# A decoder sample's attention spread over three head slots of the dense tiles' expert search

## What is computed

```python
s = jnp.einsum('bqhd,bkhd->bhqk', q, k) * scale   # + forget bias, + mask
p = jax.nn.softmax(s, axis=-1)
o = jnp.einsum('bhqk,bkhd->bqhd', p, v)           # for each of the 8 samples
...
q  = (xb @ w_pq).reshape(128, 8, 256)             # _peer, one 128-frame block
s1 = jnp.einsum('thd,hnd->thn', q[..., :128], sub_keys[0])
s2 = jnp.einsum('thd,hnd->thn', q[..., 128:], sub_keys[1])
v1, i1 = lax.top_k(s1, 16);  v2, i2 = lax.top_k(s2, 16)
cand = v1[..., :, None] + v2[..., None, :]
sv, si = lax.top_k(cand.reshape(128, 8, 256), 16)
```

## Time and profile before

| | us |
|---|---|
| median of 3 runs (1957.52 to 1961.84) | 1957.95 |
| the profiled execution, whole time | 1963.01 |
| its span, first to last instruction | 1961.2 |
| busy: PE 90%, DVE 82%, ACT 41%, POOL 50% of the span | |
| the stage: first query matmul to the turn of the choices | 357.1 to 605.8 |

### The profile page before, as it was taken

One profiled execution on the slowest core, in us unless ns is written; L12 is line 12 of the kernel. 1 busy time (PEld: TensorE's weight loads), 2 busy tenths in 40 slices (PEclk: granted clock), 3 DMA queues, 4 the chain that ended last, 5 costly groups with the idle time before them and its releaser, 6 DMA issues.

```text
span 1961.2 us, 28368 instructions
## 1 busy us (share of the span) xinstructions
PE 1766.0 (90%) x9239; PEld 1486.5 (76%) x9239; DVE 1603.1 (82%) x3321; ACT 803.9 (41%) x1314; POOL 974.2 (50%) x779
## 2 busy tenths in 40 slices
PE   6999989877795876739999999999999999999998
PEld 4883554656644866629999999999999999999997
DVE  5306462477758799999999999999999999999999
ACT  4312661333314554623444344344434443444443
POOL 0004000033213022157777777777777777777773
PEclk8999999888777989969999999999999999999999
DMA  6110303333212443549999999999999999999996
GB/s 246 43 63 2 129 1 123 115 100 100 72 43 86 153 142 124 172 165 417 415 398 412 389 393 400 411 391 392 407 405 393 391 405 403 390 400 407 395 393 273
DMA packets 169005, 517.87 MB, mean 264 GB/s; under 512 B 18128, under 2 KB 51856, under 8 KB 164848
## 3 DMA queue, kind: packets, MB, share of 16 engines
q0 software_dynamic: 73728, 268.47, 34.3%
q1 hardware_dynamic: 70448, 223.46, 30.0%
q10 hardware_dynamic: 24768, 25.17, 3.7%
HBM read 486.20 MB, written 30.84 MB: 264 GB/s over the span
## 4 chain that ended last, share of the span: by engine, by line
PE 77%; DVE 16%; ACT 5%; issue 2%; DMA 1%; SPq 0%; ACTq 0%; DVEq 0%
PE ps L1295 27%; PE ps L1311 9%; PE ps L1313 9%; PE ps L1312 9%; PE ps L1145 3%; DVE asel L1583 2%; DVE bsel L1576 2%; PE ps L984 2%; PE ps L985 2%; PE ps L986 2%; PE ps L1184 1%; PE ps L1233 1%; PE ps L1091 1%; PE ps L1201 1%; PE ps L1104 1%
## 5 line engine op out<-in xcount | busy, mean ns | idle before, releaser
L628 POOL DMA_INDIRECT ubuf<-in_peer_u,ix x256 | 388.3, 1517 | 156.2 <-POOL ix L673 109.1
L628 POOL DMA_INDIRECT vbuf<-in_peer_v,ix x256 | 406.4, 1588 | 78.9 <-issue 77.7
L1311 PE MATMUL ps<-hh,uh 128*128 128x384 f32 x1024 | 346.4, 338 | 18.9 <-DVEq L1694 18.9
L1313 PE MATMUL ps<-hh,ul 128*128 128x384 f32 x1024 | 345.6, 337 | 0.0
L1312 PE MATMUL ps<-hl,uh 128*128 128x384 f32 x1024 | 344.2, 336 | 0.0
L1706 DVE SCALAR_TENSOR_TENSOR ubuf<-ubuf,h2Y 128x1024 f32<-128x1024 f32 x256 | 302.7, 1220 | 3.5 <-DMA ubuf<-in_peer_u,ix 2.8
L930 ACT ACTIVATE vh<-vb 128x1024 fp32r<-128x1024 f32 x128 | 135.9, 1062 | 299.0 <-PE ps L1295 287.6
L1295 PE MATMUL ps<-vl,acth 128*128 128x512 f32 x774 | 243.2, 395 | 0.0
L1295 PE MATMUL ps<-vh,actl 128*128 128x512 f32 x774 | 242.6, 394 | 0.0
L1295 PE MATMUL ps<-vh,acth 128*128 128x512 f32 x774 | 242.6, 394 | 0.0
L1311 PEld LDWEIGHTS ps<-hh,uh 128*128 128x128 f32 x1024 | 193.7, 189 | 25.3 <-issue 19.7
(11 more groups left out here) (367 smaller groups left out, 2948.4 us busy)
## 6 DMA issues: line engine op xcount, KB each, us to landing
ub<-in_peer_uT SPq DMA_DIRECT2D x130, 512.0 KB, 6.7
vb<-in_peer_v SPq DMA_DIRECT2D x129, 512.0 KB, 6.5
gbuf<-gate_matrix SPq DMA_DIRECT2D x68, 384.0 KB
gate_matrix<-stage ACTq DMA_DIRECT2D x12, 2048.0 KB, 7.8
wpqX<-in_wpq SPq DMA_DIRECT2D x8, 1024.0 KB, 4.9
wpqY<-in_wpq SPq DMA_DIRECT2D x8, 1024.0 KB, 5.0
w_oX<-in_w_o SPq DMA_DIRECT2D x4, 1024.0 KB, 8.1
kTs<-in_past_k SPq DMA_DIRECT2D x8, 512.0 KB, 4.0
```

The lines of the kernel that those rows point to most:

```text
L628: nc.gpsimd.indirect_dma_start(out=dst[slot][:, e, :], out_offset=None, in_=t_in[table], in_offset=bass.IndirectOffsetOnAxis(ix[:, slot, e ...
L1311: mm(ps[:, 6 + slot, 0:NTD], uh[slot][:, k], hh[:, k], start=(k == 0), stop=False)
L1313: last = mm(ps[:, 6 + slot, 0:NTD], ul[s][:, k], hh[:, k], start=False, stop=(k == KD - 1))
```

## The change

No instruction is added or dropped; three queues get another order.

- PE: `transpose_probabilities(h - 1)` moves behind `key_scores(h)`, to the end of the head. `sample_values` of sample h - 2 moves between the halves of the queries of head h, so a sample's values come one head later than its transposition. `turn_rows(h - 2)` moves behind the queries.
- ACT: `copy_rows(h - 2)` moves ahead of `copy_queries`, `copy_scores` ahead of `copy_transposed`.
- DVE: `normalise` leaves the end of the iteration. For a sample of odd number it stands in the next iteration behind four items of `half_choices`, for one of even number inside `pair_choices` behind its first eight items (a scaling, the candidates, six maxima). Both halves of `low_weights` stand ahead of `row_max`. Behind a pair (h = 3, 5, 7), the first half and `copy_out` stand behind only four items.

```diff
@@ ACT
             for h in range(PH):
                 if h + 1 < PH:
                     round_weights(h + 1, 0)
+                if h >= 2:
+                    copy_rows(h - 2)
                 copy_queries(0, h)
                 if h + 1 < PH:
                     round_weights(h + 1, 1)
+                copy_scores(0, h)
                 if h >= 1:
                     copy_transposed(FIRST + h - 1)
-                copy_scores(0, h)
                 exponentials(FIRST + h)
-                if h >= 1:
-                    copy_rows(h - 1)
+            copy_rows(DB - 2)
@@ PE
             for h in range(PH):
-                queries(0, h, (lambda: turn_rows(h - 2)) if h >= 2 else None)
+                queries(0, h, (lambda: sample_values(h - 2)) if h >= 2 else None)
+                if h >= 2:
+                    turn_rows(h - 2)
                 scores(FIRST + h)
+                key_scores(0, h)
                 if h >= 1:
                     transpose_probabilities(FIRST + h - 1)
-                key_scores(0, h)
-                if h >= 1:
-                    sample_values(h - 1)
+            sample_values(DB - 2)
             project_out(TD)
@@ DVE
             low_weights(1, 0)
-            normalise(FIRST)
             low_weights(1, 1)
             for h in range(1, PH + 1):
                 items = half_choices(0, h - 1)
-                some(items, 14)
-                if h >= 2:
+                behind_pair = h % 2 == 1 and h > 1
+                some(items, 4)
+                if not behind_pair:
+                    normalise(FIRST + h - 1)
+                else:
+                    if h + 1 < PH:
+                        low_weights(h + 1, 0)
+                    copy_out(FIRST + h - 2)
+                some(items, 8)
+                if not behind_pair and h + 1 < PH:
+                    low_weights(h + 1, 0)
+                some(items, 4)
+                if not behind_pair and h >= 2:
                     copy_out(FIRST + h - 2)
                 if h + 1 < PH:
-                    low_weights(h + 1, 0)
-                some(items, 6)
+                    low_weights(h + 1, 1)
+                some(items, 4)
                 if h < PH:
                     row_max(FIRST + h)
-                some(items, 4)
-                if h < PH:
-                    normalise(FIRST + h)
-                if h + 1 < PH:
-                    low_weights(h + 1, 1)
                 finish(items)
...
                 if h % 2 == 0:
-                    finish(pair_choices(0, h // 2 - 1))
+                    items = pair_choices(0, h // 2 - 1)
+                    some(items, 8)
+                    if h < PH:
+                        normalise(FIRST + h)
+                    finish(items)
```

## The result

The changed kernel takes 1929.49 us (median of four runs, 1927.88 to 1932.49) beside 1957.74 for the kernel before: a ratio of 0.9844, 95% interval 0.9831 to 0.9857, or 28 to 33 us. Measured again beside the experiments, it gave 0.9841 (0.9827 to 0.9854). The forecast was a gain of 37.6 us, to 1920. The profiled execution took 1932.49, its span 1930.7.

A forecast was written before the change was run, and what follows sets the result against it. Neither PE nor DVE fills a stretch; they wait for each other in turn. 418.5 + 41 + 41 + 45.7 puts the last `onehot2X` at 546.2, 37.6 us earlier: 1957.95 - 37.6 = 1920 us, range 1910 to 1936.

The forecast's parts named there:

- the stage: Part of the kernel from 357.1 to 605.8 us, holding all that the change moves; forecast gain 37.6 us.
- the first milestone: DVE's first of four `onehot2X`, one per pair of heads: forecast at 418.5 instead of 424.02, 5.5 us earlier.
- the forecast's own band of 1915 to 1926: Whole kernel time around the forecast of 1920 us; chance 0.60.
- a clock that stays low long: Rival: PE's half clock lasts 15.4 us after each wait, gain only 23.7, 1934 us; chance 0.15 for 1926 to 1938.
- the middle stretches: First to second and second to third `onehot2X` of DVE: forecast 41 us each, before 49.4 and 54.4.
- the walk: Adding measured lengths along the new waits, from one `onehot2X` (time T) to the next: T + 39.9 at full clock.
- half a `low_weights`: DVE term behind a pair, ahead of `copy_out`: 1.15 us, so PE's transposes start at T + 6.3, T being the `onehot2X`.
- nothing waits for new keys: Forecast wait of PE before scores of samples 4 and 6: arrives T + 17.8, goes on T + 20.0 after POOL's decode.
- DVE's 38 us: DVE's work from one `onehot2X` to the next, taken as unchanged; nothing shorter than 38 us was held possible.
- The rule: GpSimd shares SBUF access with VectorE; a denser DVE would stretch POOL's decode, 6 us more, 1926 us; rival's chance 0.05.
- the same 6 us of half clock after each wait: PE's clock loss behind its wait before the transposes: cost 0.9 us per middle pair, last forecast 45.7 instead of 42.7.
- the last stretch: Third to last `onehot2X` of DVE, with the output projection on PE: forecast 45.7 us, 42.7 at full clock.

The follow-up runs named there:

- the faster kernel: Changed kernel with both `low_weights` halves and `copy_out` ahead of the one-hots, new keys ahead of the decode, odd normalising behind 12 items: 1924.17 us (0.9807).

## Why the prediction was right and wrong

**Sign, place and rough size were right.** The gain is all in the stage, and the first milestone came 6.1 us earlier for the 5.5 forecast. But 1929.5 lies above the forecast's own band of 1915 to 1926, in the one of 1926 to 1938 that was kept for a clock that stays low long. In the middle stretches it was not that: with the clock held at 1.00 they stayed at 43.1. The number fell into that band for another reason, and it lies inside the range because the range was wide.

**Half of the miss lies outside the walk.** Of the 9.4 us between the forecast gain and the measured one (28.3 by the medians), the stage accounts for 4.5. The late start of the stage is 1.7 (in the second profile of the changed kernel it began at 357.05 instead of 358.84, so this varies from one execution to the next), the time behind it 0.9. The other 2.3 come from taking the gain of one execution off the median: that execution lay 5.3 us above the median before and 3.0 after.

**The step that failed is a term of the middle stretches: half a `low_weights`, 1.15 us in the walk from T to T + 6.1.** It was priced by the row at 412.00, 1.22 long, when POOL was idle. In its new place it stands beside POOL's product and took 3.60, so the transposes began at T + 8.6 instead of T + 6.3. The second half, which the walk left inside DVE's 38 us, took 3.15. With both, DVE has 41.9 us of work, its gaps of about 1 us between dependent instructions come on top, and no path through PE matters any more. In the run without POOL's products, the same order gave 40.0 and 38.9, and PE's wait was 3.9: with that term at its price, the walk, forecast at 39.9 without a loss of clock, came out. That is in part luck, for two terms changed places: nothing waits for new keys there (2.2 us in the walk), and PE still comes to those scores at T + 20.2 and T + 19.1 instead of T + 17.8, made late by half clock.

**The row for the right price was there.** The earlier trace rows hold the same instruction twice: 1.22 at 412.00 and 1.59 at 433.15. The longer one is the one beside POOL's work. I should have asked why, and taken its worst case, the length of POOL's instruction (4.80 and 3.45), as the upper bound. The first half alone would then have been bounded at 1.2 + 4.8.

**The rule was weighed in one direction only.** The earlier trace rows show a product of 4.80 beside 3.45, and the prediction made of it that POOL would be stretched by a denser DVE. POOL's two products hardly changed (4.79 and 3.51), and its first decode as a whole, from the first product to the first copy of new keys, took 18.17 us instead of 17.20; what was stretched was DVE. The trace of the changed kernel shows both directions: the first product, asked for while `onehotX` was being built, ends 3.35 us after DVE has gone on from `onehotX` to the reciprocal (422.94 to 426.29), a product's own length; and each half of `low_weights` ends one length after the product. POOL's additions behind each product, which meet that half, took 4.31 and 4.34 here and 3.45 in the third pair, where no half is left.

The Trainium skill, SBUF — State Buffer, section SBUF: two separate sides, says just this: the port pair that VectorE and GpSimd share is an exclusive lock, and the instruction that starts first keeps it for its whole length while the other is blocked. The trace agrees, 3.60 and 3.15 for 1.22.

**The wait for the new keys** (2 us in the forecast) is not in the trace after, for PE came to those scores at T + 21.5, behind the keys. Where the halves were moved away it appeared as 0.25 and 0.40: PE, slowed by its half clock, was there at about T + 19, not T + 17.8. It was a true wait but a small one.

**The clock** was costed with the same 6 us of half clock after each wait. In the middle stretches it was 3.2 and some 4.5 us and cost nothing, since DVE was the bound (filling the wait left 43.1). In the last stretch it was more. These stretches of the changed kernel begin where the transposes do:

```profile
428.20:431.40 3.20, 3.20 (x13) 3.04 (x14) 3.17 (x25) 0.85 (x2) 2.96 (x6) 0.51 0.00 0
...
510.62:513.50 2.88, 1.94 (x14) 1.34 (x18) 2.85 (x22) 0.85 (x2) 2.80 (x2) 0.50 0.02 6
513.50:518.00 4.50, 4.50 (x31) 2.66 (x21) 4.27 (x26) 1.37 (x2) 4.26 (x6) 0.50 0.01 2
518.00:524.00 6.00, 6.00 (x13) 2.42 (x12) 5.85 (x24) 1.13 (x5) 5.53 (x6) 0.83 0.00 0
```

(The clock is the number before the last two; 0.50 is 1.2 GHz.) After a wait of 6.29 us it stood at half for some 3.2 us; after one of 3.71, with a second one of 0.94 close behind, for some 9. The forecast went by the length of the wait, and that was the wrong guide. In the last stretch 3.0 us were forecast and 4.0 measured, most of what that stretch missed.

**Costed at nothing** were the moves of `copy_rows`, `sample_values` and the loads, and none of them shows. Not named at all was that the row maxima come behind both halves of `low_weights`. Here it cost nothing, because DVE was the bound; in the faster kernel it cost 3 us.

**The odd normalising** meets POOL as well. For sample 7, in the last stretch, it takes 2.58 us in the changed kernel and 0.63 in the run without POOL's products, which has the same order:

```profile
519.20 2.58 DVE L1438 TENSOR_SCALAR probS<-probS,stat 128x272 f32<-128x272 f32 x2
...
510.13 0.63 DVE L1439 TENSOR_SCALAR probS<-probS,stat 128x272 f32<-128x272 f32 x2
```

The prediction left it inside DVE's 38 us. It has one tensor as input; no run here shows why it is held up and the searches are not.

## What to carry to other kernels

When an instruction is moved, price it by a row that has the same neighbours on the other engines, not by its shortest row: if one instruction has two lengths in a trace, find out what ran beside the longer one before using the shorter. A stall of this kind carries no idle time; it shows as busy time that grew with the same number of instructions, so compare busy times of a stretch, not only waits. When an engine's busy time nears the length of the stretch, a shorter wait elsewhere gives nothing, as `copy_out` ahead of the first half showed.

## What the runs showed of the hardware

A VectorE instruction with two SBUF operands, 1.22 us long, waited out GpSimd's running product, and its length in the trace includes that: 3.60, 3.15, 2.94 and 3.82, each ending about 1.1 us after the product. A pair of scalings with one SBUF tensor as input took 2.58 beside GpSimd's work and 0.63 without it. VectorE's searches and replacements ran beside the same products at their usual 0.28. Half clock after a wait lasted 3.2 us once and about 9 another time, the longer one after the shorter wait; matmuls that nobody reads, put into the wait, kept the clock at 1.00 in the middle stretches, where they gained nothing, and raised it to 0.92 in the last one, where PE was the bound and they gained 4.0 us.
